# Mean squares of the prompt's heads on eight columns, and the sample's value sums stacked in one bank

## The chip, the cores and the metric

The kernel runs on one core of a Trainium2 chip. The metric is the time of one execution on the device, in microseconds. One layer of a decoder is computed for 256 prompt tokens and 8 sample tokens (264 in all) with the same weights.

## The reference, cut to what matters

The change touches two pieces: the RMS normalisation of the prompt's differential attention, and the sums of attention weights times cached values for the eight samples.

```python
def _diff_attend(q, k, v, q_pos, k_pos, lam, lam_init, subln_g):
    ...
    attn = p[:, :, 0] - lam * p[:, :, 1]
    o = jnp.einsum('bhqk,bkhe->bqhe', attn.astype(v.dtype), v).astype(jnp.float32)
    o = o * lax.rsqrt(jnp.mean(o * o, -1, keepdims=True) + RMS_EPS) * subln_g * (1.0 - lam_init)
    return o.astype(v.dtype)
...
def _layer_tail(x, a, o, ga, gb, w_a_up, w_b_up, w_out, ...):
    merged = jax.nn.sigmoid(ga) * (a @ w_a_up) + jax.nn.sigmoid(gb) * (o @ w_b_up)
    h = _layer_norm(ALPHA * x + merged @ w_out, ln1_g, ln1_b)
```

There are 4 differential heads of 128 values each. A sample attends to 256 cached keys in 2 pages and to its own new key.

## The kernel before, in words

Activations lie transposed: 128 features of a tile on the partitions, tokens along the columns. The order on each engine is written out by hand, and semaphores join the engines. Work runs in stages: 30 tiles of the input projection, the attention of prompt and samples with 16 gate tiles between its parts, the up projections, the output projection, a layer norm, and then the PEER experts (128 tiles of `experts_u`, 128 of `experts_v`), which are most of the time.

Attention writes to three PSUM banks in rotation. `UNIT_ORDER` lists the units; unit n uses bank 5 + n modulo 3. On TensorE `fill(name)` waits until the unit three before it has been copied out; `await_unit` and `await_drained` are the other sides of it. The stage of the change is this, in TensorE's order:

- gate tiles 14 and 15 (L1334), then 24 transposes of the sparse attention (L1453, six units that ScalarE copies out at L627), then the sparse value products of the prompt (L1467, L1469), copied out at L632.
- `sampT`: the samples' attention weights are transposed (L1496, L1498). VectorE copies them into `samp_pad` (L1019), where each sample has 32 columns of its own, eight of them filled.
- `rms0`, `rms1` (L1505): a 128x128 matrix of ones times the squares of `o_diff` (made by ScalarE at L663), 512 columns each. Every partition then holds the sum for each head and token. VectorE adds epsilon (L1039), takes the reciprocal over all 1024 columns (L1063), ScalarE takes the root (L687), VectorE multiplies (L1047) and scales (L1048).
- `samp_diff0`, `samp_diff1`, `samp_sparse0`, `samp_sparse1` (L1517): four samples per unit, each on 32 columns of the array, writing 32 partitions of the bank. `pick` (L1055) masks each out of its bank, and `samp_o` (L1527) turns the rows back into columns: 16 products with 8 columns.
- `rms2` (L1533): the same normalisation for the eight samples, 32 columns.
- the up projections (L1545, L1546, L1549), from `sparse_hi`, `sparse_lo`, `diff_hi`, `diff_lo`, which hold a rounded part and the rest (`diff_hi` at L689, `sparse_lo` at L1075, `diff_lo` at L1082), and from `up_hi`, `up_lo` (L678, L1069).

On VectorE the queue after `sampT` is: evacuate rms0 and rms1, reciprocal, `up_low` twice, `sparse_lo`, `pick(0)`, multiply, scale, `diff_lo`, `pick(1)`, and the samples' short steps. On ScalarE: the samples' exponentials (L615), two output copies, `up_high` twice, `sparse_hi`, root, `diff_hi`. GpSimd issues the loads of value pages (L449).

A product of two float32 operands shows as two matmul records in the trace, a transpose as one.

Of the kernel before, what the change touches and what calls it, by code (L numbers as in the profile page):

```python
# [27 lines left out]
ALU = mybir.AluOpType  # L28
ACT = mybir.ActivationFunctionType
# [47 lines left out]
CONSTS = C_OWNER + 2 * TS  # L77
# [21 lines left out]
              + [f"diffT{u}" for u in range(3)] + ["diff_o0", "diff_o1"]  # L99
# [9 lines left out]
def build_program(nc, x_t, weights, experts_u, experts_v, k_cache, v_cache,  # L109
                  page_table, sub_keys, params, consts, alibi, sample_bias, kv_out, y_out):  # L110
    with ExitStack() as ctx:
# [9 lines left out]
        def rounded(name, over, at, words):  # L121
# [9 lines left out]
            pad_zero pad_filled out_sample_ready rms_square rms_recip rms_root up_b_filled up_b_free  # L131
# [89 lines left out]
        samp_rows = s_sparse[:, 1024:3072].rearrange("p (n h e) -> p n h e", n=2, h=2)  # L221
# [22 lines left out]
        top8 = c(3 * 8)  # L244
        phase = c.at
# [313 lines left out]
        def _(act):  # L559
# [120 lines left out]

            up_high(0, 0)
# [4 lines left out]
            act.wait_ge(S["rms_recip"], 1)  # L686
            act.activation(s_diff[:, RMS:RMS + 4 * TP], s_diff[:, RMS:RMS + 4 * TP], ACT.Sqrt).then_inc(S["rms_root"], 1)  # L687
# [140 lines left out]
        def _(dve):  # L828
# [163 lines left out]

            dve.wait_ge(S["sample_scored"], 2)
# [43 lines left out]
            def mean_squares(u, at, n):  # L1037
                await_unit(dve, f"rms{u}")
                drain_unit(dve.tensor_scalar(s_diff[:, RMS + at:RMS + at + n], bank(f"rms{u}")[:, 0:n], 1.0 / P, EPS,  # L1039
                                             ALU.mult, ALU.add), f"rms{u}")  # L1040
                await_drained(dve, f"rms{u}")

            def rms_apply(t0, t1):

                o = o_diff[:, :, t0:t1]
                roots = s_diff[:, RMS + 4 * t0:RMS + 4 * t1].rearrange("p (j t) -> p j t", j=4)
                chain(dve.tensor_tensor(o, o, roots, ALU.mult))  # L1047
                chain(dve.tensor_scalar(o, o, par[:, P_SUBLN:P_SUBLN + 1], 1.0 - LAM_INIT, ALU.mult, ALU.mult))  # L1048

            def pick(n, kind, mask, heads):  # L1050

                for g in range(2):
                    name = f"samp_{kind}{g}"
                    await_unit(dve, name)
                    drain_unit(dve.tensor_tensor(samp_rows[:, n, g, :].rearrange("p (h e) -> p h e", h=heads),  # L1055
                                                 bank(name).rearrange("p (h e) -> p h e", h=heads),
                                                 cst[:, mask:mask + heads].unsqueeze(2).to_broadcast([P, heads, 512 // heads]),
                                                 ALU.mult), name)
# [19 lines left out]
            dve.wait_ge(S["rms_root"], 1)  # L1078
            rms_apply(0, TP)
# [18 lines left out]
            mean_squares(2, 4 * TP, 4 * TS)  # L1098
            dve.reciprocal(s_diff[:, RMS + 4 * TP:RMS + 4 * T], s_diff[:, RMS + 4 * TP:RMS + 4 * T])\
                .then_inc(S["rms_recip"], 1)  # L1100
            dve.wait_ge(S["rms_root"], 2)
            rms_apply(TP, T)
# [221 lines left out]
        def _(pe):  # L1324
# [159 lines left out]
            gate_tile(EARLY_GATES + 3)  # L1484
            pe.wait_ge(S["sparse_attn"], 2)
# [22 lines left out]
            for n, kind in enumerate(("diff", "sparse")):  # L1508
                pe.wait_ge(S["pad_filled"], 2 * n + 2)
                for h in range(2):  # L1510
                    name = f"samp_{kind}{h}"
                    fill(name)
                    for b in range(4 * h, 4 * h + 4):
                        pe.wait_ge(vc_loaded[b], 32)
                    for g in range(PAGES):
                        for q in range(4):
                            last = pe.matmul(bank(name)[32 * q:32 * q + 32, :], samp_pad[:, n, g, 4 * h + q, :],  # L1517
                                             vbuf[4 * h + q][kind][:, g, :], start=(g == 0), stop=(g == PAGES - 1))
                    last.then_inc(S["unit_filled"], 1)

            fill("samp_o")
            for n, kind in enumerate(("diff", "sparse")):
                for h in range(2):
                    await_drained(pe, f"samp_{kind}{h}")
                for j in range(4):
                    for h in range(2):
                        last = pe.matmul(bank("samp_o")[:, 32 * n + 8 * j:32 * n + 8 * (j + 1)],  # L1527
                                         samp_rows[:, n, h, j * P:(j + 1) * P], cst[:, C_OWNER + TS * h:C_OWNER + TS * (h + 1)],
# [272 lines left out]
```

## Time and profile before

| | |
|---|---|
| median of 3 runs | 1243.46 us |
| lowest, highest | 1240.25, 1245.73 us |
| profiled execution, its time | 1244.86 us |
| profiled execution, its span | 1242.9 us |
| mean granted TensorE clock | 0.97 |
| TensorE matmul busy | 1165.0 us, 94% |
| VectorE, ScalarE, GpSimd busy | 829.7, 524.8, 448.7 us |

Times of rows are in microseconds from the span's start. A granted clock of 1.00 is 2.4 GHz and 0.50 is 1.2 GHz. Busy time of TensorE comes from modelled ends of pipelined matmuls, so the distance between starts says more than the duration of one.

### The profile page before, as it was taken

The page shows a single profiled execution, that of the slowest core. Times are in us where ns is not written, and L with a number is a line of the kernel's source. Part 1 is how long each engine was busy: PE and PEld are TensorE (multiplying, and loading weights), DVE is VectorE, ACT ScalarE, POOL GpSimd, SP SyncE. Part 2 cuts the span into 40 slices and gives each one's busy share as a digit, 9 for nine tenths or more (in the row PEclk, how much of TensorE's full clock was granted, in tenths as well). Part 3 has the DMA queues.
Part 4 walks back from the last instruction along what each step waited for, and adds up shares of the span by engine and source line. Part 5 has one row for each costly group of instructions (what it writes and reads, how often), then busy time and mean ns, then how long its engine had stood idle before and what let it go on. Part 6 is the DMA issues. An engine that isn't in the chain of part 4 may idle for free.

```text
span 1242.9 us, 25892 instructions
## 1 busy us (share of the span) xinstructions
PE 1165.0 (94%) x9133; PEld 1113.8 (90%) x9133; DVE 829.7 (67%) x1827; ACT 524.8 (42%) x822; POOL 448.7 (36%) x237
## 2 busy tenths in 40 slices
PE   7998879799699999999999999999999999999996
PEld 7996756388599999989999999998999999999995
DVE  4447716546599999975666677746666666666665
ACT  4445224424334666765444444443333333333333
POOL 1100224022366999996666666663000000000000
PEclk9998897879899999999999999999999999999999
DMA  7772666314133454544334434444555555555551
GB/s 250 250 283 115 215 217 237 101 56 158 58 136 134 156 176 159 185 153 152 136 135 136 138 138 142 140 138 166 179 177 185 176 179 186 174 180 184 174 182 35
DMA packets 55175, 201.08 MB, mean 162 GB/s; under 512 B 6208, under 2 KB 7232, under 8 KB 54752
## 3 DMA queue, kind: packets, MB, share of 16 engines
q1 hardware_dynamic: 49472, 177.30, 41.4%
q0 software_dynamic: 5376, 23.01, 5.6%
q8 instruction: 17, 0.28, 0.1%
q10 hardware_dynamic: 288, 0.32, 0.1%
q14 instruction: 22, 0.18, 0.0%
HBM read 197.22 MB, written 3.38 MB: 161 GB/s over the span
## 4 chain that ended last, share of the span: by engine, by line
PE 79%; issue 7%; POOL 6%; DVE 6%; ACT 2%; POOLq 0%; DMA 0%; ACTq 0%; DVEq 0%
PE psum L1673 20%; PE psum L1682 10%; PE psum L1615 8%; PE psum L1610 7%; PE psum L1611 7%; POOL w_lo L548 5%; PE psum L1644 5%; PE psum L1350 5%; PE psum L1354 4%; PE psum L1351 4%; PE psum L1334 1%; PE psum L1389 1%; PE psum L1591 1%; PE psum L1570 1%; PE psum L1549 1%
## 5 line engine op out<-in xcount | busy, mean ns | idle before, releaser
L548 POOL TENSOR_TENSOR w_lo<-ring,w_hi 128x1024 fp32r<-128x1024 f32 x128 | 335.9, 2632 | 116.4 <-ACT w_hi L767 116.3
L1610 PE MATMUL psum<-h_hi,w_hi 128*128 128x264 f32 x1024 | 260.6, 290 | 0.0
L1673 PE MATMUL psum<-cells_hi,w_hi 128*128 128x264 f32 x1024 | 254.8, 285 | 3.0 <-ACT w_hi L814 3.0
L1611 PE MATMUL psum<-h_lo,w_hi 128*128 128x264 f32 x1024 | 254.6, 285 | 0.0
L1673 PE MATMUL psum<-cells_lo,w_hi 128*128 128x264 f32 x1024 | 254.5, 284 | 0.0
L814 ACT ACTIVATE w_hi<-ring 128x1024 fp32r<-128x1024 f32 x128 | 135.7, 1061 | 235.4 <-PE psum L1673 235.2
L767 ACT ACTIVATE w_hi<-ring 128x1024 fp32r<-128x1024 f32 x128 | 135.4, 1059 | 170.3 <-PE psum L1611 135.0
L1673 PEld LDWEIGHTS psum<-cells_hi,w_hi 128*128 128x128 f32 x1024 | 193.1, 189 | 3.3 <-issue 2.9
L1673 PEld LDWEIGHTS psum<-cells_lo,w_hi 128*128 128x128 f32 x1024 | 193.4, 189 | 0.0
L1611 PEld LDWEIGHTS psum<-h_lo,w_hi 128*128 128x128 f32 x1024 | 193.2, 189 | 0.0
L1610 PEld LDWEIGHTS psum<-h_hi,w_hi 128*128 128x128 f32 x1024 | 192.9, 188 | 0.3 <-issue 0.2
L1300 DVE TENSOR_TENSOR w_lo<-ring,w_hi 128x1024 fp32r<-128x1024 f32 x128 | 157.0, 1227 | 0.0
L1615 PE MATMUL psum<-h_hi,w_lo 128*128 128x264 f32 x1024 | 147.7, 286 | 8.9 <-POOL w_lo L548 8.7
L1615 PEld LDWEIGHTS psum<-h_hi,w_lo 128*128 128x128 f32 x1024 | 133.9, 189 | 11.6 <-POOL w_lo L548 11.6
L1682 PE MATMUL psum<-cells_hi,w_lo 128*128 128x264 f32 x1016 | 144.1, 284 | 0.0
L522 POOL TENSOR_TENSOR ring<-ring,small 128x264 f32<-128x264 f32 x4 | 3.0, 785 | 380.8 <-ACT small L719 380.8
L1682 PEld LDWEIGHTS psum<-cells_hi,w_lo 128*128 128x128 f32 x1016 | 132.0, 189 | 0.0
L1291 DVE CAST cells_hi<-arena 128x264 fp32r (+1 forms) x128 | 39.8, 311 | 125.8 <-PE psum L1682 125.8
L1350 PE MATMUL psum<-x_hi,z_hi 128*128 128x264 f32 x336 | 87.5, 295 | 10.0 <-DVE x_lo L838 8.6
L1257 DVE TENSOR_SCALAR work<-psum,work 128x128 f32<-128x128 f32 x264 | 89.7, 401 | 0.0
L1351 PE MATMUL psum<-x_lo,z_hi 128*128 128x264 f32 x336 | 85.1, 288 | 0.0
L1350 PEld LDWEIGHTS psum<-x_hi,z_hi 128*128 128x128 f32 x336 | 64.5, 192 | 14.6 <-ACT z_hi L576 8.6
(258 smaller groups left out, 1795.5 us busy)
## 6 DMA issues: line engine op xcount, KB each, us to landing
ring<-experts_u_dram SPq DMA_DIRECT2D x128, 512.0 KB, 3.2
ring<-experts_v_dram SPq DMA_DIRECT2D x128, 512.0 KB, 3.2
ring<-weights_dram SPq DMA_DIRECT2D x78, 512.0 KB, 3.4
arena<-k_cache_dram POOLq DMA_DIRECT2D x16, 576.0 KB, 6.3
arena<-v_cache_dram POOLq DMA_DIRECT2D x16, 512.0 KB, 7.4
kv_out_dram<-arena POOLq DMA_DIRECT2D x1, 2244.0 KB, 8.3
arena<-alibi_dram POOLq DMA_DIRECT2D x1, 1664.0 KB, 8.7
xt<-x_t_dram SPq DMA_DIRECT2D x2, 528.0 KB, 5.8
```

Of the source, the lines that this page charges most:

```text
L548: pool.tensor_tensor(halves_of(w_lo, k, D), raw, halves_of(w_hi, k, D), ALU.subtract)\
L767: act.activation(halves_of(w_hi, k, D), raw, ACT.Copy).then_inc(S["u_hi_made"], 1)
L814: act.activation(halves_of(w_hi, k, D), raw, ACT.Copy).then_inc(S["v_hi_made"], 1)
L1257: last = dve.tensor_scalar(p2[:, 4 * q + k, :], iota_near, slots[:, 1, t0 + k:t0 + k + 1], slots[:, 2, t0 + k:t0 + k + 1], ALU.is_equal, A ...
L1300: dve.tensor_tensor(halves_of(w_lo, k, D), raw, halves_of(w_hi, k, D), ALU.subtract)\
L1350: pe.matmul(out, part(hi, c, P), token_part(x_parts[0], c), start=(c == 0), stop=False)
L1351: pe.matmul(out, part(hi, c, P), token_part(x_parts[1], c), start=False, stop=False)
L1610: pe.matmul(out, part(hi, c, P), token_part(h_hi, c), start=(c == 0), stop=False)
L1611: last = pe.matmul(out, part(hi, c, P), token_part(h_lo, c), start=False, stop=False)
L1615: last = pe.matmul(out, part(lo, c, P), token_part(h_hi, c), start=False, stop=(c == DC - 1))
L1673: last = pe.matmul(psum[:, c, 0:T], part(hi, c, P), cells[n], start=(first and n == 0), stop=False)
L1682: last = pe.matmul(psum[:, c, 0:T], part(halves_of(w_lo, k, D), c, P), cell_part(cells_hi, k), start=False, stop=False)
```

## The change

The squares of `o_diff` become the stationary operand and a single column of ones the moving one. For each of 8 blocks of 128 (4 heads, 2 halves of the tokens) this gives one column, a sum per token on the partitions. The unit `rms0` now stands ahead of the sparse transposes. VectorE adds epsilon on 8 columns, ScalarE takes the root of 8, VectorE the reciprocal. To get the factor onto every partition, VectorE makes 8 diagonal blocks, the identity times the factor (128x1024, `rms_diag`), and TensorE multiplies them with ones (`spread0`, `spread1`); VectorE multiplies `o_diff` with the banks directly. The root stands ahead of `up_high` in ScalarE's queue, and the drain of `rms0` ahead of the sample's maxima (L995) in VectorE's.

In `samp_pad` the second four samples fill columns 8 to 15 of their 32, and both groups of four add up in one bank: two units in place of four, the same number of products, `pick` twice in place of four times, `samp_o` with 8 products in place of 16. `samp_diff` waits for the pages of all eight samples.

```diff
-              + ["sampT", "rms0", "rms1", "samp_diff0", "samp_diff1", "samp_sparse0", "samp_sparse1",
-                 "samp_o", "rms2"])
+              + ["sampT", "samp_diff", "spread0", "spread1", "samp_sparse", "samp_o", "rms2"])
...
# ScalarE
+            act.wait_ge(S["rms_recip"], 1)
+            act.activation(rms8, rms8, ACT.Sqrt).then_inc(S["rms_root"], 1)
             up_high(0, 0)
             up_high(0, 1)
...
-            act.wait_ge(S["rms_recip"], 1)
-            act.activation(s_diff[:, RMS:RMS + 4 * TP], s_diff[:, RMS:RMS + 4 * TP], ACT.Sqrt).then_inc(S["rms_root"], 1)
...
# VectorE, ahead of the sample's maxima
+            await_unit(dve, "rms0")
+            drain_unit(dve.tensor_scalar(rms8, bank("rms0")[:, 0:8], 1.0 / P, EPS, ALU.mult, ALU.add), "rms0")
+            await_drained(dve, "rms0")
+            dve.sem_inc(S["rms_recip"], 1)
...
-                    dve.tensor_copy(samp_pad[:, n, :, 4 * g:4 * g + 4, 0:8], pages).then_inc(S["pad_filled"], 1)
+                    dve.tensor_copy(samp_pad[:, n, :, 4 * g:4 * g + 4, 8 * g:8 * g + 8], pages).then_inc(S["pad_filled"], 1)
...
-            for u in range(2):
-                mean_squares(u, 512 * u, 512)
-            dve.reciprocal(s_diff[:, RMS:RMS + 4 * TP], s_diff[:, RMS:RMS + 4 * TP]).then_inc(S["rms_recip"], 1)
+            dve.wait_ge(S["rms_root"], 1)
+            chain(dve.reciprocal(rms8, rms8))
+            dve.tensor_tensor(rms_diag, ident.unsqueeze(1).to_broadcast([P, 8, P]),
+                              rms8.unsqueeze(2).to_broadcast([P, 8, P]), ALU.mult).then_inc(S["rms_spread"], 1)
...
-            dve.wait_ge(S["rms_root"], 1)
-            rms_apply(0, TP)
+            for u in range(2):
+                await_unit(dve, f"spread{u}")
+                o = o_diff[:, 2 * u:2 * u + 2, 0:TP]
+                drain_unit(dve.tensor_tensor(o, o, bank(f"spread{u}").rearrange("p (j t) -> p j t", j=2), ALU.mult), f"spread{u}")
+            for u in range(2):
+                await_drained(dve, f"spread{u}")
+            rms_scale(o_diff[:, :, 0:TP])
...
# TensorE, after gate tile 15
+            pe.wait_ge(S["rms_square"], 1)
+            fill("rms0")
+            for n in range(8):
+                last = pe.matmul(bank("rms0")[:, n:n + 1], s_diff[:, n * P:(n + 1) * P], ones[:, 0:1], start=True, stop=True)
+            last.then_inc(S["unit_filled"], 1)
...
# TensorE, after sampT
-            pe.wait_ge(S["rms_square"], 1)
-            for u in range(2):
-                fill(f"rms{u}")
-                pe.matmul(bank(f"rms{u}"), ones, s_diff[:, 512 * u:512 * (u + 1)], start=True, stop=True)\
-                    .then_inc(S["unit_filled"], 1)
+            def sample_values(n, kind):
+                name = f"samp_{kind}"
                 pe.wait_ge(S["pad_filled"], 2 * n + 2)
+                fill(name)
+                for b in range(TS):
+                    pe.wait_ge(vc_loaded[b], 32)
                 for h in range(2):
                     for g in range(PAGES):
                         for q in range(4):
                             last = pe.matmul(bank(name)[32 * q:32 * q + 32, :], samp_pad[:, n, g, 4 * h + q, :],
+                                             vbuf[4 * h + q][kind][:, g, :], start=(h == 0 and g == 0),
+                                             stop=(h == 1 and g == PAGES - 1))
+                last.then_inc(S["unit_filled"], 1)
+            sample_values(0, "diff")
+            pe.wait_ge(S["rms_spread"], 1)
+            for u in range(2):
+                fill(f"spread{u}")
+                pe.matmul(bank(f"spread{u}"), ones, rms_diag[:, 4 * u:4 * u + 4, :].rearrange("p n q -> p (n q)"),
+                          start=True, stop=True).then_inc(S["unit_filled"], 1)
+            sample_values(1, "sparse")
...
-                    for h in range(2):
-                        last = pe.matmul(bank("samp_o")[:, 32 * n + 8 * j:32 * n + 8 * (j + 1)],
-                                         samp_rows[:, n, h, j * P:(j + 1) * P], cst[:, C_OWNER + TS * h:C_OWNER + TS * (h + 1)],
-                                         start=(h == 0), stop=(h == 1))
+                    last = pe.matmul(bank("samp_o")[:, 32 * n + 8 * j:32 * n + 8 * (j + 1)],
+                                     samp_rows[:, n, j * P:(j + 1) * P], cst[:, C_OWNER:C_OWNER + TS], start=True, stop=True)
```

The masks `C_PAIR`, `C_HEAD` and `C_OWNER` move with the rows, and `rms_apply` loses its first part to the lines above.

## Rows read from the trace of the kernel before

**Rows 1.** The page, part 1: busy time by engine.
```profile
PE 1165.0 (94%) x9133; PEld 1113.8 (90%) x9133; DVE 829.7 (67%) x1827; ACT 524.8 (42%) x822; POOL 448.7 (36%) x237
```

**Rows 2.** The chain of waits, 214 to 228: start, us, what.
```profile
214.24 7.32 PE psum L1334 x32
...
222.03 3.04 ACT work L627 x6
...
227.51 0.17 DVE small L1001
```

**Rows 3.** Timeline of TensorE: start, us, instructions, idle before.
```profile
221.39 2.92 PE L1453 MATMUL psum<-cst,work 128*128 128x128 f32 x24
225.13 0.66 PE L1467 MATMUL psum<-work 128*64 128x256 f32 x4 [0.81 <-ACT work L627]
...
227.56 0.44 PE L1469 MATMUL psum<-work 128*64 128x128 f32 x4
229.37 0.34 PE L1496 MATMUL psum<-cst,small 64*128 64x64 f32 x2 [1.37 <-DVE small L1010]
...
231.38 3.78 PE L1505 MATMUL psum<-arena,cst 128*128 128x512 f32 x4 [1.10 <-DVE small L1024]
235.09 6.52 PE L1517 MATMUL psum<-arena,work 128*32 128x512 f32 x48
246.54 3.64 PE L1517 MATMUL psum<-arena,work 128*32 128x512 f32 x16 [4.93 <-DVE work L1055]
250.12 7.00 PE L1527 MATMUL psum<-cst,work 128*128 128x8 f32 x32
...
260.39 0.59 PE L1545 MATMUL psum<-sparse_hi,up_hi 128*128 128x264 f32 x1 [1.82 <-DVEq L1110]
```

**Rows 4.** Timeline of VectorE, 231 to 250.
```profile
231.49 0.43 DVE L1034 TENSOR_TENSOR small<-small,arena 64x32 f32<-64x32 f32 x2
...
235.99 6.55 DVE L1063 RECIPROCAL arena<-arena 128x1024 f32<-128x1024 f32 x1
242.46 2.29 DVE L1069 TENSOR_TENSOR up_lo<-ring,up_hi 128x1024 fp32r<-128x1024 f32 x2
244.67 1.22 DVE L1075 TENSOR_TENSOR sparse_lo<-arena,sparse_hi 128x1024 fp32r<-128x1024 f32 x1
245.81 1.28 DVE L1055 TENSOR_TENSOR work<-psum,cst 128x512 f32<-128x512 f32 x2
247.01 1.22 DVE L1047 TENSOR_TENSOR arena<-arena 128x1024 f32<-128x1024 f32 x1
248.26 0.75 DVE L1048 TENSOR_SCALAR arena<-arena,par 128x1024 f32<-128x1024 f32 x1
```

**Rows 5.** Windows of 1 us: busy by engine, TensorE's granted clock third from last.
```profile
121.00:122.00 1.00, 0.53 (x4) 0.00 (x0) 1.00 (x2) 1.00 (x3) 0.00 (x0) 0.79 0.00 0
230.00:231.00 1.00, 0.28 (x3) 0.14 (x2) 0.68 (x5) 1.00 (x2) 0.00 (x0) 0.83 0.56 213
237.00:238.00 1.00, 1.00 (x12) 0.12 (x4) 1.00 (x1) 0.00 (x0) 0.00 (x0) 0.76 0.00 0
244.00:245.00 1.00, 0.00 (x0) 0.00 (x0) 1.00 (x2) 0.00 (x0) 0.00 (x0) 0.65 0.30 53
250.00:251.00 1.00, 1.00 (x9) 0.89 (x5) 0.81 (x1) 0.16 (x1) 0.00 (x0) 0.50 0.00 0
264.00:265.00 1.00, 1.00 (x7) 1.00 (x6) 0.12 (x1) 0.00 (x0) 0.00 (x0) 0.61 0.00 0
```

**Rows 6.** Timeline of VectorE, the sample's maxima.
```profile
214.28 0.42 DVE L995 SCALAR_TENSOR_TENSOR small<-psum,sbias 64x257 f32<-64x257 f32 x1 [2.03 <-PE psum L1480]
```

**Rows 7.** Timeline of ScalarE.
```profile
231.48 1.28 ACT L687 ACT_TABLE_LOAD   x1
...
249.10 1.06 ACT L689 ACTIVATE diff_hi<-arena 128x1024 fp32r<-128x1024 f32 x1 [5.46 <-DVEq L1080]
```

**Rows 8.** Timeline of GpSimd, the last value page issued.
```profile
204.55 0.72 POOL L449 DMA_DIRECT2D arena<-v_cache_dram  x1 [0.41 <-issue]
```

More of the change, by code:

```diff
@@ L98 @@
               + [f"diff{u}" for u in range(6)] + ["isum"] + [f"sparse{u}" for u in range(6)]
[L99 removed]
+              + [f"diffT{u}" for u in range(3)] + ["diff_o0", "diff_o1", "rms0"]
               + [f"sparseT{u}" for u in range(6)] + ["sparse_o0", "sparse_o1"]
[L101 to L102 removed]
+              + ["sampT", "samp_diff", "spread0", "spread1", "samp_sparse", "samp_o", "rms2"])
 UNIT = {name: n for n, name in enumerate(UNIT_ORDER)}
@@ L1035, in _, with rms_scale @@
             chain.settle()
[L1037 to L1047, printed above, removed]
+            def rms_scale(o):
                 chain(dve.tensor_scalar(o, o, par[:, P_SUBLN:P_SUBLN + 1], 1.0 - LAM_INIT, ALU.mult, ALU.mult))
             def pick(n, kind, mask, heads):
[L1052 to L1058, printed above, removed]
-            for u in range(2):
-                mean_squares(u, 512 * u, 512)
-            dve.reciprocal(s_diff[:, RMS:RMS + 4 * TP], s_diff[:, RMS:RMS + 4 * TP]).then_inc(S["rms_recip"], 1)
+                name = f"samp_{kind}"
+                await_unit(dve, name)
+                drain_unit(dve.tensor_tensor(samp_rows[:, n, :].rearrange("p (h e) -> p h e", h=heads),
+                                             bank(name).rearrange("p (h e) -> p h e", h=heads),
+                                             cst[:, mask:mask + heads].unsqueeze(2).to_broadcast([P, heads, 512 // heads]),
+                                             ALU.mult), name)
+            dve.wait_ge(S["rms_root"], 1)
+            chain(dve.reciprocal(rms8, rms8))
+            dve.tensor_tensor(rms_diag, ident.unsqueeze(1).to_broadcast([P, 8, P]),
+                              rms8.unsqueeze(2).to_broadcast([P, 8, P]), ALU.mult).then_inc(S["rms_spread"], 1)
             def up_low(i, m):
@@ L1097, in _ @@
                               ALU.subtract).then_inc(S["sparse_lo_made"], 1)
-            mean_squares(2, 4 * TP, 4 * TS)
-            dve.reciprocal(s_diff[:, RMS + 4 * TP:RMS + 4 * T], s_diff[:, RMS + 4 * TP:RMS + 4 * T])\
-                .then_inc(S["rms_recip"], 1)
+            roots = s_diff[:, RMS + 4 * TP:RMS + 4 * T]
+            await_unit(dve, "rms2")
+            drain_unit(dve.tensor_scalar(roots, bank("rms2")[:, 0:4 * TS], 1.0 / P, EPS, ALU.mult, ALU.add), "rms2")
+            await_drained(dve, "rms2")
+            dve.reciprocal(roots, roots).then_inc(S["rms_recip"], 1)
             dve.wait_ge(S["rms_root"], 2)
-            rms_apply(TP, T)
+            o = o_diff[:, :, TP:T]
+            chain(dve.tensor_tensor(o, o, roots.rearrange("p (j t) -> p j t", j=4), ALU.mult))
+            rms_scale(o)
             dve.sem_inc(S["out_sample_ready"], 1)
@@ L1501, in _ @@
             await_drained(pe, "sampT")
-            pe.wait_ge(S["rms_square"], 1)
-            for u in range(2):
-                fill(f"rms{u}")
-                pe.matmul(bank(f"rms{u}"), ones, s_diff[:, 512 * u:512 * (u + 1)], start=True, stop=True)\
-                    .then_inc(S["unit_filled"], 1)
-            for n, kind in enumerate(("diff", "sparse")):
+            def sample_values(n, kind):
+                name = f"samp_{kind}"
                 pe.wait_ge(S["pad_filled"], 2 * n + 2)
+                fill(name)
+                for b in range(TS):
+                    pe.wait_ge(vc_loaded[b], 32)
                 for h in range(2):
[L1511 to L1514, printed above, removed]
                     for g in range(PAGES):
```

19 lines of the change are left out of this document (9 added, 10 removed).

## The prediction

> **What bounds the kernel now.** The page's first part comes first: TensorE is busy for 94% of the span and no other engine for more than 67% [rows 1]. So outside its own waits a change pays only through what TensorE has to do, and inside them through what it waits for. The chain of waits around the edit shows the order of events: gate tile 15 ends at 221.56, the sparse transposes follow, ScalarE copies six units, loads a table and does the sample's exponentials, and VectorE takes over at 227.51 [rows 2]. The timeline of TensorE then shows the stage itself. The sample transposes start at 229.37. After them come the two rms products of 512 columns (231.38 to 235.09), the diff value sums and the first half of the sparse ones (235.09, for 6.52 us), an idle 4.93 us that a copy by VectorE at L1055 ends, the last 16 value instructions (3.64 us), the 32 instructions of samp_o (7.00 us), rms2, and at 260.39 the first up product [rows 3]. From 231.38 to 260.39 is 29.0 us. VectorE's timeline says why TensorE idles: between the first rms product and the copy that frees the bank lies the reciprocal over 1024 columns, 6.55 us, with up_low and sparse_lo behind it [rows 4]. The bank rotation carries the wait: samp_sparse1 needs samp_diff1 drained, and pick(0, "diff") is queued behind the reciprocal on VectorE. The granted clock is the last view: each row is a mean of the two levels 1.00 (2.4 GHz) and 0.50 (1.2 GHz), so its share dates the step. It falls at 230.7, rises at 237.5, falls again at 244.3 inside the idle stretch, samp_o begins at 0.50, and it rises at 264.8, after the up products have begun [rows 5].
>
> **The change, part by part, on the path.**
>
> *Added ahead of the stage.* The mean squares now take 8 products of one column each, with 128x128 stationary slices, between gate tile 15 and the sparse transposes. That place is on the chain [rows 2], so all of their time counts. The nearest row is samp_o: 16 products of 8 columns are 32 instructions in 7.00 us, 0.219 us each at half clock, where weight loads of 128x128 fill the time [rows 3, 5]. The clock at 221 is full, so I take half, 0.11 us, for 16 instructions: 1.7 us. Transposes at full clock give 2.9 us / 24 = 0.12 [rows 3], 1.9 us. Bounds: 0 (if hidden behind ScalarE's evacuation of the gate) and 3.5 us (half clock). VectorE's drain of 8 columns comes next, some 0.2 us (the reciprocal of two columns takes 0.17 [rows 2]); it is over before the third transpose unit wants its bank, since ScalarE takes 3.04 us for the six units [rows 2]. VectorE had nothing to do there but the sample's maxima (from L995 on, four instructions of about 0.4 us, before at 214.28 [rows 6]); they move to about 225.2. ScalarE wants them after its copies and table load, at 221.56, plus 1.7, four transposes (0.5), 3.04 and 1.28, which is 228.1 [rows 2, 3, 7]. Cover is 2.9 us; without it the difference would be paid in full. So everything to the start of the stage shifts by 1.7, and 231.38 becomes 233.1.
>
> The Trainium skill ("TensorE: Matmul & The Clock Gate", section "Back-to-back issue gap") gives small products a floor of about 25 ns from start to start, and adds that in streams with weight loads the spacing is set by both. By the floor alone the 16 instructions would be an estimated 0.4 us instead of 1.7. Samp_o's row speaks against it: 0.219 us for 8 columns.
>
> *TensorE in the stage.* The rms products at its head go (3.71 us). Then:
> - samp_diff, now 32 instructions in a row. At half clock they take 3.64 / 16 = 0.227 us each by the last row of them [rows 3], so 0.113 at full clock. When does the clock rise? Before it took 6.1 us from 231.38, and 4.4 us from 260.39 [rows 3, 5]; I take 5.2: 23 instructions, then 9 at 0.113, in all 6.2 us. It ends at 239.3.
> - spread0 and spread1: 4 instructions of 512 columns, before 0.93 each at half clock (3.71 / 4), so 0.45 at full: 1.8 us, to 241.1. They wait for rms_spread. VectorE makes it from a reciprocal of 8 columns (0.2) and a product of 128x1024 (1.22, as L1047 [rows 4]) right after its small sample work at 231.92 + 1.7; done at 235.1, 4 us before it is wanted. Its root on ScalarE needs the table load, 1.28 [rows 7], now ahead of up_high: up_hi and sparse_hi come some 1.5 us later, and VectorE reaches up_low only at 235.1. Nothing is late.
> - samp_sparse, 32 x 0.113 = 3.6, to 244.7. Its bank needs the diff copy: VectorE has done up_low (2.29) and sparse_lo (1.22) at 238.6, then copies samp_diff at 239.3 to 240.0.
> - samp_o: 8 products in place of 16, 16 instructions at full clock. Half (0.9 us) can run once samp_sparse is issued, the other half waits for pick(1).
>
> *VectorE in the stage.* Gone: the reciprocal (6.55), two evacuations of 512 columns and their waits, two of four copies of 0.64, one product of 1.22. New: 0.2, 1.22, and two products of 128x512 out of the bank of about 0.64 each (as L1055 [rows 4]). From spread1 at 241.1: product 0.64, scale 0.75, diff_hi on ScalarE 1.1, diff_lo 1.2 (as sparse_lo), pick(1) 0.64 [rows 4, 7]: 245.6. This chain now sets the end, 0.9 us past TensorE. With the last 8 instructions of samp_o (0.9) it is 246.5.
>
> *Tail.* From samp_o's end to the first up product was 257.12 to 260.39, 3.27 us of short steps [rows 3]. It is not edited: 249.8.
>
> **The sum.** 260.39 - 249.8 = 10.6 us. In parts: TensorE's stage to the end of samp_o is 13.4 instead of 25.7 us, 12.3 less; 1.7 is given back ahead of it. The up products follow and everything after waits for TensorE or for what TensorE releases; no transfer with a clock of its own is in the chain, so I carry the gain to the end. The profiled execution took 1244.86 us with a span of 1242.9; 1244.9 - 10.6 = 1234.3. The median of the runs is 1243.46, 1.4 below it, so 1233 is my time, 0.85% less.
>
> **Rivals.**
> 1. *The clock falls before the stage.* Between gate tile 15 and the sparse value products (L1467) TensorE now has 5.3 us of one-column products and transposes, before 3.6. After 3 us of idling in two places (227.9 to 230.7, 241.6 to 244.4) it fell [rows 3, 5]. If it falls here, the products of 2.9 us take up to twice that, of which 1.4 us fit before the sample transposes: 1.5 us lost, and samp_diff may start colder. Against: the clock held through 24 transposes. Time 1235 to 1236.
> 2. *The clock does not rise during the value sums.* They use 32 columns of the array at a time, and the 3.64 us of them at 246.54 raised nothing [rows 3, 5]. Then samp_diff takes 7.3, spread 3.7, samp_sparse 7.3 from 233.1 to 251.4; with the copy (0.64) and half of samp_o (1.75) it is 253.8, the up products start at 257.1, a gain of 3.3: 1240. Against: the earlier scores of the same 128x32 form (L1429) had it rise at 121.4 [rows 5], and here the stretch is longer and without a gap.
> 3. *The clock is still full at the first up product.* Before, 4.4 us of them ran at half, so up to 2.2 us more: 1231. Against: the samp_o products at half clock and the waits of the tail never raised it, and here the tail still idles.
> 4. *Small products are nearly free*, as the floor would have it: 1.3 us less ahead, 0.7 less in samp_o: 1231. For it nothing in the rows. This is the rule weighed above.
> 5. *It does nothing in the end*: the stage is shorter, but a later wait on something other than TensorE takes it back. 1243. VectorE at 67% and ScalarE at 42% leave room [rows 1].
> 6. *Slower: the wait for all eight value pages.* samp_diff now waits for pages 0 to 7 at once. The last page is issued at 204.55 [rows 8] and nothing wants it before 231. If it landed after 233.1, each us would be paid; the gain is gone at 243.7 and a slowdown of 0.5% begins at 249.9. A landing at 252 would give 1252. Against: 28 us of lead.
>
> **How the numbers follow.** Forecast 0.61; rival 1 0.13, rival 2 0.07, rival 3 0.08, rival 4 0.03, rival 5 0.05, rival 6 0.03. The forecast's own range is 1230.5 to 1236 (the clock's rise between 4.4 and 6.1 us is 0.9 us, the added products -1.7 to +1.8 of their 1.7, runs before spread over 5.5 us). The range takes in rivals 1, 3 and 4 and the way to rival 2: 1229 to 1239, and leaves out some 1.5 in 10. A measurement of this kernel tells 0.5%, 6.2 us, from no change, so faster is below 1237.2: forecast, rivals 1, 3 and 4 almost whole, 0.82; the same is rivals 2 and 5 and a rest, 0.14; slower 0.04.
>
> **What would show it.** Right: L1063 gone with its 6.55 us, no idle of more than 0.5 us on TensorE between the sample transposes and samp_o, samp_o in 16 instructions near 0.11 us, the first up product near 249.8, and the same distance from there to the end as before. The added products show as 16 instructions of one column at 221.6, 0.11 us each. Wrong if the clock in 234 to 245 stays at 0.50, if L1467 after them runs at half, if the table load or the maxima hold up ScalarE at 228, or if the up products start earlier and a later wait grows.

## Result and the profile after

| | before | changed |
|---|---|---|
| median (11 runs each) | 1242.76 us | 1231.9 us |
| lowest, highest | 1239.6, 1248.3 | 1229.7, 1237.65 |
| ratio, 95% interval | | 0.9919 [0.9899, 0.9939] |
| span of the profiled execution | 1242.9 | 1227.7 |

The change makes the kernel 0.8% faster; 1233 us was forecast. The two profiled spans differ by more, 15.2 us. Where that comes from is read off three marks that both traces have: the first product of gate tile 14, the first up product, and the first product of the output projection.

| stretch | before | changed | difference |
|---|---|---|---|
| start to gate tile 14 | 214.17 | 209.22 | -4.95 |
| gate tile 14 to the first up product | 46.22 | 34.96 | -11.26 |
| to the output projection | 29.89 | 30.22 | +0.33 |
| to the end | 952.6 | 953.3 | +0.7 |

The first stretch holds no edited line. In the twelve traces of this study (these two and one of each experiment) gate tile 14 begins anywhere from 208.66 to 215.07, whatever was edited behind it. So 4.95 us of the 15.2 is luck of these two executions, and the medians of the runs rightly differ by less. The edit's part is 10.9 us up to the output projection.

The timeline of TensorE in the changed kernel: start, us, line, what; L1493 is the unit of one-column products, L1521 the value sums, L1530 the spread products, L1538 samp_o, L1543 rms2.
```profile
209.22 7.39 PE L1339 MATMUL psum<-xt,ring 128*128 128x264 f32 x32
216.44 1.84 PE L1493 MATMUL psum<-cst,arena 128*128 128x1 f32 x16
218.15 2.96 PE L1458 MATMUL psum<-cst,work 128*128 128x128 f32 x24
...
226.16 0.34 PE L1506 MATMUL psum<-cst,small 64*128 64x64 f32 x2 [1.37 <-DVE small L1016]
...
228.17 5.34 PE L1521 MATMUL psum<-arena,work 128*32 128x512 f32 x32 [1.10 <-DVE small L1030]
233.44 1.99 PE L1530 MATMUL psum<-arena,cst 128*128 128x512 f32 x4
235.35 3.64 PE L1521 MATMUL psum<-arena,work 128*32 128x512 f32 x32
238.93 2.20 PE L1538 MATMUL psum<-cst,work 128*128 128x8 f32 x16
241.95 0.41 PE L1543 MATMUL psum<-arena,cst 128*128 128x32 f32 x2 [0.83 <-ACT arena L693]
244.18 0.59 PE L1555 MATMUL psum<-sparse_hi,up_hi 128*128 128x264 f32 x1 [1.82 <-DVEq L1115]
```
The idle 4.93 us of [rows 3] is gone, and so are the two rms products at the head of the stage. From the start of samp_diff to the end of samp_o nothing on TensorE waits longer than a fraction of a microsecond. Samp_o is 16 instructions in 2.20 us at full clock, a short wait between its halves included, where it was 32 in 7.00 at half.

The chain of waits of the changed kernel over the end of the stage shows what sets its end now.
```profile
233.50 1.93 PE psum L1530 x4
...
235.46 0.70 DVE arena L1077
...
236.25 0.76 DVE arena L1044
...
237.10 1.07 ACT diff_hi L690
...
238.19 0.94 DVE diff_lo L1083
...
239.33 0.69 DVE work L1050
...
240.07 1.07 PE psum L1538 x8
```
After the second spread product the chain leaves TensorE. It runs over VectorE's product and scale, ScalarE's diff_hi, diff_lo and the copy of samp_sparse, and returns for the second half of samp_o.

The granted clock of the changed kernel, third number from the end of each window of 1 us:
```profile
228.00:229.00 1.00, 0.83 (x8) 0.29 (x12) 0.87 (x6) 1.00 (x2) 0.00 (x0) 0.91 1.00 426
232.00:233.00 1.00, 1.00 (x16) 0.18 (x8) 1.00 (x2) 0.00 (x0) 0.00 (x0) 0.88 0.47 152
242.00:243.00 1.00, 0.36 (x2) 0.25 (x2) 0.74 (x3) 0.02 (x1) 0.00 (x0) 0.74 0.00 0
249.00:250.00 1.00, 1.00 (x9) 1.00 (x9) 0.07 (x1) 0.00 (x0) 0.00 (x0) 0.85 0.00 0
```
Read as in [rows 5], it falls at 228.8, when samp_diff has run for 0.65 us, rises at 232.2 (4.1 us into samp_diff), falls at 242.5 in the tail and rises at 249.3, which is 5.1 us after the first up product, against 4.4 before. Those 0.7 us more at half clock cost half their length, the +0.33 of the table. The second fall of before, at 244.3, has no counterpart: it happened in the idle time that is gone, and had put the last 16 value instructions and all of samp_o at half clock.

### The profile page after: what moved, and what is told of

Same layout as the page of the kernel before. It is cut to its first block, busy times and chain, and to the rows that moved or that the text cites. A ratio compares the mean times of both kernels' runs of the same rounds, so it can differ in the third digit from the quotient of the medians.

```text
span 1227.7 us, 25892 instructions
## 1 busy us (share of the span) xinstructions
PE 1158.3 (94%) x9133; PEld 1111.8 (91%) x9133; DVE 822.4 (67%) x1826; ACT 523.9 (43%) x822; POOL 448.1 (37%) x237
## 4 chain that ended last, share of the span: by engine, by line
PE 80%; issue 8%; POOL 6%; DVE 4%; ACT 2%; POOLq 0%; DMA 0%; ACTq 0%; DVEq 0%
PE psum L1683 20%; PE psum L1692 10%; PE psum L1625 8%; PE psum L1620 7%; PE psum L1621 7%; POOL w_lo L549 5%; PE psum L1355 5%; PE psum L1654 5%; PE psum L1356 4%; PE psum L1359 4%; PE psum L1339 1%; PE psum L1601 1%; PE psum L1394 1%; PE psum L1580 1%; PE psum L1559 1%
```

## The experiments

All distances are in microseconds from the first product of gate tile 14, in one profiled execution of each kernel. That makes them independent of the first stretch. The changed kernel, e1 and e7 have the same code up to the value sums and agree to 0.01 us there. A step of the clock that falls elsewhere can move a distance by more, up to 1.8 us in e2, so each is read together with the clock. The ratios are to the kernel before, from runs on the same chip. The intervals of e1, e3 to e6 and e8 overlap that of the changed kernel, so how those differ from it is read from the distances alone. "Up" is the first up product, "output" the first product of the output projection. In the kernel before and in e2 the two rms products stand ahead of the value sums. Where gate tile 15 was moved away, gate tile 14 is the first half of the old row L1339.

| kernel | value sums begin | up | output | ratio [95%] |
|---|---|---|---|---|
| before | 20.92 | 46.22 | 76.11 | |
| changed | 18.95 | 34.96 | 65.18 | 0.9919 [0.9899, 0.9939] |
| e1, rms part alone | 18.95 | 36.74 | 66.23 | 0.9935 [0.9910, 0.9961] |
| e2, stacking alone | 19.12 | 40.66 | 71.00 | 0.9975 [0.9954, 0.9996] |
| e3, rms0 in the gap | 17.64 | 33.45 | 63.10 | 0.9903 [0.9874, 0.9932] |
| e4, extra products | 19.42 | 34.70 | 62.64 | 0.9901 [0.9872, 0.9930] |
| e5, gate tile 15 later | 18.36 | 33.00 | 62.64 | 0.9891 [0.9859, 0.9923] |
| e6, e3 and extra products | 17.65 | 32.93 | 60.87 | 0.9885 [0.9852, 0.9918] |
| e7, copy first | 18.95 | 34.72 | 65.06 | profile only |
| e8, e5 and extra products | 18.31 | 32.95 | 60.78 | 0.9882 [0.9846, 0.9919] |
| e9, e8 with rms0 earlier | 16.24 | 30.88 | 58.74 | 0.9863 [0.9839, 0.9888] |
| e10, e9 and copy first | 16.24 | 30.63 | 58.46 | 0.9871 [0.9847, 0.9894] |

**e1: the rms part alone.** The changed kernel with the sample's part as it was:
```diff
-                    dve.tensor_copy(samp_pad[:, n, :, 4 * g:4 * g + 4, 8 * g:8 * g + 8], pages).then_inc(S["pad_filled"], 1)
+                    dve.tensor_copy(samp_pad[:, n, :, 4 * g:4 * g + 4, 0:8], pages).then_inc(S["pad_filled"], 1)
...
+                for h in range(2):
+                    name = f"samp_{kind}{h}"
+                    fill(name)
...
+                    for h in range(2):
+                        last = pe.matmul(bank("samp_o")[:, 32 * n + 8 * j:32 * n + 8 * (j + 1)],
+                                         samp_rows[:, n, h, j * P:(j + 1) * P], cst[:, C_OWNER + TS * h:C_OWNER + TS * (h + 1)],
+                                         start=(h == 0), stop=(h == 1))
```


> The mean squares on 8 columns with the spread product, but the sample's value sums in four units and samp_o with 16 products as before. Distances are measured from the first product of gate tile 14 to the first up product: 46.2 us in the kernel before, 35.0 in the changed one. My theory (the reciprocal over 1024 columns held the bank and with it TensorE, and is most of the gain): VectorE has two more copies of 0.64 us and samp_o 16 instructions more, of which half or so lie on the path, so 37.0 us, a gain of 9 over the kernel before, ratio 0.993. Rival (stacking is most of the gain, because it takes two bank waits away): 42 us or more, ratio 0.997.

Measured: 36.74 us, 9.5 less than before. The timeline of TensorE in e1:
```profile
230.10 5.34 PE L1522 MATMUL psum<-arena,work 128*32 128x512 f32 x32 [1.10 <-DVE small L1030]
235.36 1.99 PE L1530 MATMUL psum<-arena,cst 128*128 128x512 f32 x4
237.28 3.65 PE L1522 MATMUL psum<-arena,work 128*32 128x512 f32 x32
240.86 3.75 PE L1540 MATMUL psum<-cst,work 128*128 128x8 f32 x32
```
The four units run without a wait between them. Without the reciprocal, the bank rotation of before costs nothing. The clock matters too: the same 32 instructions of samp_o took 7.00 us at half clock in the kernel before and 3.75 here, so 3.3 of the 9.5 us come from a clock that no longer falls ahead of them.

What stacking adds is 1.8 us. Samp_o begins 10.76 us after the value sums in both kernels and ends 1.55 us later in e1, whose chain of waits stays on TensorE:
```profile
237.35 3.58 PE psum L1522 x32
240.93 3.70 PE psum L1540 x32
```
So VectorE's two extra copies are covered here. The other 0.23 us are in the tail: rms2 runs at half clock in e1 (0.63 us) and at full in the changed kernel (0.41 us).

**e2: the stacking alone**, on the kernel before:
```diff
-                for h in range(2):
-                    name = f"samp_{kind}{h}"
-                    fill(name)
...
+                name = f"samp_{kind}"
+                fill(name)
+                for b in range(TS):
+                    pe.wait_ge(vc_loaded[b], 32)
...
-                    for h in range(2):
-                        last = pe.matmul(bank("samp_o")[:, 32 * n + 8 * j:32 * n + 8 * (j + 1)],
-                                         samp_rows[:, n, h, j * P:(j + 1) * P], cst[:, C_OWNER + TS * h:C_OWNER + TS * (h + 1)],
-                                         start=(h == 0), stop=(h == 1))
+                    last = pe.matmul(bank("samp_o")[:, 32 * n + 8 * j:32 * n + 8 * (j + 1)],
+                                     samp_rows[:, n, j * P:(j + 1) * P], cst[:, C_OWNER:C_OWNER + TS], start=True, stop=True)
```


> The value sums stacked in one bank per kind and samp_o with 8 products, but the mean squares by two products of 512 columns and the reciprocal over 1024 columns as before. My theory: TensorE no longer waits for the copy behind the reciprocal and is through its value sums at about 243.4 on the clock of the kernel before, but VectorE's row of reciprocal, up_low, sparse_lo, copy, product, scale, diff_lo and copy then sets the end: 42.3 us from gate tile 14 to the first up product, a gain of 4, ratio 0.997. The two parts would then gain 9 and 4 alone and 11.3 together. Rival (the two parts are independent and add up): 44 us, a gain of 2.

Measured: 40.66 us, 5.6 less than before. Neither number fits, the forecast was 42.3. TensorE's timeline and a window of e2:
```profile
228.14 1.99 PE L1504 MATMUL psum<-arena,cst 128*128 128x512 f32 x4 [1.10 <-DVE small L1024]
230.06 7.08 PE L1516 MATMUL psum<-arena,work 128*32 128x512 f32 x64
241.61 1.85 PE L1525 MATMUL psum<-cst,work 128*128 128x8 f32 x8 [4.47 <-DVE work L1054]
246.44 1.87 PE L1525 MATMUL psum<-cst,work 128*128 128x8 f32 x8 [2.99 <-DVE work L1054]
```
```profile
239.00:240.00 1.00, 0.00 (x0) 0.00 (x0) 1.00 (x2) 0.00 (x0) 0.00 (x0) 0.95 0.27 90
```
The mechanism is as expected: all 64 value instructions in one go, then TensorE waits twice for VectorE's copies. The size is off because in this execution the clock stayed at 1.00 from before sampT to 239.9. The rms products took 1.99 us and not 3.78, so the reciprocal began 1.8 us earlier, counted from gate tile 14. Those 1.8 us are luck of this execution: with them it would have been an estimated 42.5, near the forecast, and the twelve runs show 3.1 us less than before (0.5 to 5.7 by the interval). So the parts gain 9.5 and about 4 alone (5.6 in this trace) and 11.3 together. The sum of the parts is more than the whole because both remove the same idle time.

**e3: the one-column products in a gap.** From ahead of the sparse transposes to behind the sparse value products, where TensorE waited for the sample's chain; in `UNIT_ORDER` "rms0" moves to between "sparse_o1" and "sampT", and VectorE drains it ahead of its wait for sampT:
```diff
-            pe.wait_ge(S["rms_square"], 1)
-            fill("rms0")
-            for n in range(8):
-                last = pe.matmul(bank("rms0")[:, n:n + 1], s_diff[:, n * P:(n + 1) * P], ones[:, 0:1], start=True, stop=True)
-            last.then_inc(S["unit_filled"], 1)
             pe.wait_ge(S["sparse_attn"], 2)
...
             outputs("sparse", 8, HD)
+            pe.wait_ge(S["rms_square"], 1)
+            fill("rms0")
+            for n in range(8):
+                last = pe.matmul(bank("rms0")[:, n:n + 1], s_diff[:, n * P:(n + 1) * P], ones[:, 0:1], start=True, stop=True)
+            last.then_inc(S["unit_filled"], 1)
```


> The changed kernel with the eight one-column products moved behind the sparse value products of the prompt, where TensorE stood idle for 1.81 us before the sample transposes, and VectorE's drain of them ahead of its wait for sampT. My theory (their 1.7 us ahead of the sparse transposes are paid in full): 33.3 us from gate tile 14 to the first up product, 1.7 less than the changed kernel; over the kernel before a gain near 12.5, ratio 0.990. Rival (the products delay the sample transposes or the root on ScalarE comes too late for the diagonal blocks): 34.5 or more.

Measured: 33.45 us, 1.51 less than the changed kernel, 1.7 expected. The timeline of TensorE in e3:
```profile
227.15 0.44 PE L1474 MATMUL psum<-work 128*64 128x128 f32 x4
227.52 1.95 PE L1498 MATMUL psum<-cst,arena 128*128 128x1 f32 x16
229.39 0.33 PE L1506 MATMUL psum<-cst,small 64*128 64x64 f32 x2
...
231.40 4.91 PE L1521 MATMUL psum<-arena,work 128*32 128x512 f32 x32 [1.10 <-DVE small L1030]
```
The products fill the gap of 1.81 us and hold the sample transposes up by 0.43 (15.63 from gate tile 14, 15.20 in the kernel before). So the move itself gains 1.31 us, the difference at the start of the value sums, and not 1.7. The total comes closer by luck: the clock rose 2.6 us into samp_diff (at 234.0) and not 4.1, which takes 0.43 off, and rms2 at half clock puts 0.23 back.

**e4: what the half clock costs.** Six products that nobody reads, into a bank that is unused in this stage:
```diff
+            def warm(count):
+                for _ in range(count):
+                    pe.matmul(psum[:, 4, :], ones, cst[:, 0:512], start=True, stop=True)
+            warm(2)
             pe.wait_ge(S["samp_attn"], 2)
...
+            warm(1)
             await_drained(pe, "sampT")
...
+            warm(1)
             pe.wait_ge(S["rms_square"], 2)
...
+            warm(2)
             pe.wait_ge(S["sparse_lo_made"], 2)
```


> The changed kernel with six extra products of 512 columns whose result nobody reads, two ahead of the sample transposes, one ahead of the value sums, one behind samp_o and two ahead of the first up product; they fill TensorE's idle times. Nothing that the kernel needs is changed. It measures what the half clock costs in this stage. My theory: the value sums run at full clock from the start (3.6 us in place of 5.3), but VectorE's up_low and sparse_lo then hold the chain, so only 0.6 us of it reaches the first up product; the first up products run at full clock too, 2.5 us less. From gate tile 14 to the first product of the output projection 62.2 us against 65.2 in the changed kernel. Rival (the clock falls all the same in the tail, or the extra products delay the short steps): 64.5 to 66.

Measured: 62.64 us to the output projection, 2.54 less than the changed kernel. In its timeline the value sums take 3.64 us in place of 5.34. They begin 0.47 us later than in the changed kernel, because the two extra products ahead of the sample transposes hold those up. Then TensorE waits 0.59 us ahead of samp_sparse:
```profile
233.38 3.64 PE L1528 MATMUL psum<-arena,work 128*32 128x512 f32 x32
236.95 1.99 PE L1537 MATMUL psum<-arena,cst 128*128 128x512 f32 x4
239.53 3.64 PE L1528 MATMUL psum<-arena,work 128*32 128x512 f32 x32 [0.59 <-issue]
```
The row names no releaser. Samp_sparse needs the bank of samp_diff, and VectorE's timeline has the copy that frees it (L1050) behind sparse_lo, ending at 239.43. So it is VectorE, as forecast:
```profile
237.61 1.22 DVE L1071 TENSOR_TENSOR sparse_lo<-arena,sparse_hi 128x1024 fp32r<-128x1024 f32 x1
238.75 0.68 DVE L1050 TENSOR_TENSOR work<-psum,cst 128x512 f32<-128x512 f32 x1
```
The first up product gains only 0.26; the rest is the up products at full clock. The clock is 1.00 in every window from 225 to 262. (The trace had 954.6 us from there to the end, 1.3 more than the changed kernel, so the ratio shows less. That stretch varied from 950.1 to 955.5 over the twelve traces.)

**e5: gate tile 15 into the gap**, on e3:
```diff
             gate_tile(EARLY_GATES + 2)
-            gate_tile(EARLY_GATES + 3)
...
+            gate_tile(EARLY_GATES + 3)
             await_drained(pe, "sampT")
...
# ScalarE
-            evac_gate(EARLY_GATES + 3)
...
+            evac_gate(EARLY_GATES + 3)
             act.wait_ge(S["diff_normed"], 1)
```


> The kernel of e3 with gate tile 15 moved behind sampT on TensorE, and its sigmoid on ScalarE behind sparse_hi. The gate tile (3.66 us) no longer stands ahead of the sparse transposes, and fills the time in which TensorE waited for sampT's copies and VectorE worked through up_low. My theory (the stage is a chain of short steps with TensorE free in between, so real work belongs there): the value sums start at 16.5 us from the first product of gate tile 14 in place of 17.6 and run at full clock, 31.0 us to the first up product in place of 33.45, 60.6 to the output projection in place of 63.1; ratio to the kernel before 0.988. Rival (the extra table loads for the late sigmoid delay ScalarE's steps in the tail, or VectorE's chain is the bound and not TensorE): 33 us or more to the first up product.

Measured: 33.0 us. My theory missed by 2. The timeline of TensorE and two windows of e5:
```profile
225.27 1.95 PE L1497 MATMUL psum<-cst,arena 128*128 128x1 f32 x16
...
227.99 5.51 PE L1339 MATMUL psum<-xt,ring 128*128 128x264 f32 x16
233.43 3.64 PE L1521 MATMUL psum<-arena,work 128*32 128x512 f32 x32
```
```profile
228.00:229.00 1.00, 1.00 (x4) 0.86 (x4) 0.87 (x6) 1.00 (x2) 0.00 (x0) 0.65 1.01 426
231.00:232.00 1.00, 1.00 (x4) 0.83 (x3) 1.00 (x2) 0.86 (x1) 0.00 (x0) 0.65 0.00 0
```
The clock fell at 228.3, as the gate tile began, and came back at 231.7. The tile took 5.5 us and not 3.7, and the value sums waited for it. So the rival's number came true, but hardly for its reasons. VectorE was idle for 2.55 us before its copy of samp_diff, so it was not the bound. The late sigmoid does put a table load of 1.28 us into the chain of the tail, and by the lengths of the tails it costs 0.1 us here and 0.3 in e8 (3.37 us from the end of samp_o to the first up product, 3.06 in e6).

**e6: e3 with four extra products.** As e4, without the two ahead of the sample transposes.

> The kernel of e3 with the four later extra products of e4: one ahead of the value sums, one behind samp_o and two ahead of the first up product, none ahead of the sample transposes. My theory (what e4 gained, it gained in the tail, where the up products then start at full clock): 33.3 us from gate tile 14 to the first up product as in e3, and 60.8 to the output projection in place of 63.1; ratio 0.988. Rival (the one-column products ahead of the sample transposes do not hold the clock and the extra products behind samp_o alone cannot either, so that it falls in the tail): 62.5 to 63.2.

Measured: 32.93 and 60.87; 33.3 and 60.8 were expected. With products in the tail's gaps the clock stays at 1.00 through the up products; the three in the tail are enough, as e8 shows.

The start of the stage in e6 bears on e5. From the end of the last value product of the prompt (225.94) to the first wide product behind it, the extra one, TensorE has the same 2.6 us of one-column products and sample transposes as e5 has ahead of gate tile 15. Here the clock did not fall:
```profile
225.50 0.44 PE L1474 MATMUL psum<-work 128*64 128x128 f32 x4
225.87 1.95 PE L1498 MATMUL psum<-cst,arena 128*128 128x1 f32 x16
...
228.58 1.13 PE L1504 MATMUL psum<-cst 128*128 128x512 f32 x2
```
```profile
228.00:229.00 1.00, 1.00 (x9) 0.81 (x8) 0.33 (x4) 0.89 (x2) 0.00 (x0) 1.00 0.54 205
```

**e7: the copy first**, on the changed kernel:
```diff
             dve.sem_inc(S["diff_normed"], 1)
+            pick(1, "sparse", C_HEAD, 8)
             dve.wait_ge(S["diff_hi_made"], 1)
             dve.tensor_tensor(token_cols(diff_lo, 0, TP), o_diff[:, :, 0:TP], token_cols(diff_hi, 0, TP), ALU.subtract)\
                 .then_inc(S["diff_lo_made"], 1)
-            pick(1, "sparse", C_HEAD, 8)
```


> The changed kernel with VectorE's copy of samp_sparse moved ahead of its wait for diff_hi, so that it runs before diff_lo. My theory (at the end of the stage VectorE's chain from spread1 through scale, diff_hi, diff_lo and the copy is what samp_o waits for): the copy starts when samp_sparse is filled, 0.3 to 0.4 us earlier than now, diff_lo moves behind it beside samp_o, and the first up product comes at 34.6 to 34.7 us from gate tile 14 in place of 34.96; diff_lo then ends before samp_o does. Rival (TensorE's own row sets the end): 34.96 as it is.

Measured: 34.72, 0.24 less. VectorE's timeline in e7:
```profile
238.51 0.69 DVE L1050 TENSOR_TENSOR work<-psum,cst 128x512 f32<-128x512 f32 x1 [2.06 <-PE psum L1521]
239.12 1.22 DVE L1084 TENSOR_TENSOR diff_lo<-arena,diff_hi 128x1024 fp32r<-128x1024 f32 x1
240.36 0.19 DVE L1092 TENSOR_TENSOR arena<-psum,small 128x32 f32<-128x32 f32 x1
```
The copy now waits for TensorE, and the next short step stands behind diff_lo in VectorE's queue. VectorE's chain was the last by a quarter of a microsecond and no more.

**e8: e5 with three extra products in the tail.**

> The kernel of e5 with the three extra products in the tail (one behind samp_o, two ahead of the first up product), as in e6. My theory: both gains add up, 31.0 us from gate tile 14 to the first up product and 58.5 to the output projection, against 46.2 and 76.1 in the kernel before; the rest of the kernel unchanged at 952 to 954 us; ratio to the kernel before 0.986. Rival (a later stage takes part of it back): the rest of the kernel grows by 1 us or more.

Measured: 32.95 and 60.78, the rest 954.3. Both effects add up (62.64 less 1.86), but from e5's lower start: gate tile 15 again took 5.46 us.

**e9: the one-column products between transposes and value products**, on e8:
```diff
             transposes("sparse", s_sparse, 8, lambda h: h)
+            pe.wait_ge(S["rms_square"], 1)
+            fill("rms0")
+            for n in range(8):
+                last = pe.matmul(bank("rms0")[:, n:n + 1], s_diff[:, n * P:(n + 1) * P], ones[:, 0:1], start=True, stop=True)
+            last.then_inc(S["unit_filled"], 1)
             await_drained(pe, "sparseT5")
             outputs("sparse", 8, HD)
-            pe.wait_ge(S["rms_square"], 1)
-            fill("rms0")
-            for n in range(8):
-                last = pe.matmul(bank("rms0")[:, n:n + 1], s_diff[:, n * P:(n + 1) * P], ones[:, 0:1], start=True, stop=True)
-            last.then_inc(S["unit_filled"], 1)
```


> The kernel of e8 with the eight one-column products taken out of the gap ahead of the sample transposes and put between the sparse transposes and the sparse value products, where TensorE waits 0.81 us for ScalarE's copies; VectorE drains them behind the sample's maxima. It asks why gate tile 15 took 5.4 us in e5 and e8 in place of 3.66 and came to be what the value sums wait for. My theory (the clock fell at 228.3 in e5 because the one-column products ahead of the sample transposes are followed by short steps; with the value products closer to the gate tile it stays full): gate tile 15 takes 3.7 us, the value sums start at 16.6 us from the first product of gate tile 14 in place of 18.3, the first up product comes at 31.2 in place of 32.95 and the output projection at 59.0 in place of 60.8. Rival (the clock falls all the same, since the chip sees one-column products and transposes as idling wherever they stand): 32.9 and 60.7, or later, with the sparse value products at half clock.

Measured: 16.24, 30.88 and 58.74, each within 0.4 of the theory. TensorE's timeline in e9:
```profile
215.85 1.92 PE L1494 MATMUL psum<-cst,arena 128*128 128x1 f32 x16
...
220.13 0.44 PE L1474 MATMUL psum<-work 128*64 128x128 f32 x4
220.99 0.33 PE L1505 MATMUL psum<-cst,small 64*128 64x64 f32 x2 [0.42 <-DVE small L1016]
...
221.82 3.83 PE L1339 MATMUL psum<-xt,ring 128*128 128x264 f32 x16
```
The gate tile takes 3.83 us, here and in e10, with the clock at 1.00; it took 5.51 and 5.46 in e5 and e8. Of the 2.07 us by which the value sums begin earlier than in e8, 1.63 are the gate tile and 0.44 the closed gap. Between the end of the last value product and the gate tile lie 1.3 us here and 2.7 in e5. The theory's numbers came true, but its reason is not shown: e6 has the order of e5 and held the clock, and e2 held it over 3.4 us. In the seven traces in which it fell at this place, it fell 2.6 to 4.2 us after the last value product. That fits a shorter stretch being safer, and no more.

**e10: e9 with the copy first.**

> The kernel of e9 with VectorE's copy of samp_sparse ahead of diff_lo, as in e7. Theory: it takes 0.25 us more off, as it did in the changed kernel, so 0.25 less than e9 to the first up product; ratio to the kernel before 0.985. Rival (TensorE with samp_sparse is the last in this order, since the value sums start earlier than VectorE's work ends): no difference from e9.

Measured: 30.63, 0.25 less, as expected. Its ratio lies inside e9's interval; 0.25 us is below what the runs tell. The intervals of e9 and e10 lie just below the changed kernel's 0.9919 [0.9899, 0.9939]; each is against the kernel before on its own chip.

## Why the prediction was right

It was right in sign, size and mechanism: e1 shows that the mean squares were most of it, and e2 that with the reciprocal in place TensorE still waits for VectorE. Point by point:

- *The added products, 1.7 us, in full on the chain*: 16 instructions from 216.61 to 218.29 in the chain, 1.68. The start of the stage moved by 1.74 (17.21 to 18.95). e3 took them off the chain and began the value sums 1.31 earlier. The pace is 0.105 us each. The floor of about 25 ns that the Trainium skill gives ("TensorE: Matmul & The Clock Gate", section "Back-to-back issue gap") is not what binds here. The remark in the same section of the Trainium skill that in a stream both operations set the spacing agrees with the trace: the sixteen weight loads lie back to back in 1.98 us. The Trainium skill (same page, section "LDWEIGHTS (loading the stationary operand)") gives columns / 1.2 in nanoseconds for a weight load, an estimated 107 for 128 columns. The trace agrees at full clock, and not at half, where [rows 3] have 0.219 us for each product with its weight load.
- *VectorE's maxima and ScalarE's table load are covered*: the maxima ended at 220.3, ScalarE wanted them at 223.2. The root ran at 226.73, VectorE used it at 228.75. The cover of 2.9 was right.
- *samp_diff 6.2 us*: 5.3. The clock was still full for its first 0.65 us, where the sum had it at half from the start, and it rose 4.1 us in and not 5.2. This is the term that was off most, by 0.9. The rise is a matter of the execution: it came 2.6 us into samp_diff in e3.
- *Spread 1.8*: 1.93. *samp_sparse 3.6*: 3.58. *VectorE's chain 4.5 from the second spread product*: 235.43 to 240.02, 4.6. *Last half of samp_o 0.9*: 1.07. *Tail 3.27*: 3.04, since rms2 ran at full clock.
- *10.6 us to the first up product*: 11.26, and 10.9 to the output projection. The medians differ by 10.9, the ratio says 10.1.

Of the rivals, the first (the clock falls ahead of the stage) did not occur in the changed kernel: it was 1.00 in each window from 218 to 228. But it fell at 228.8, right behind this place, and in e5 and e8, where gate tile 15 follows, it fell as early as 2.6 us after the last value product. The second (no rise during the value sums) is refuted by the window 232 to 233, the third (a warm tail) by the window 242 to 243; e4, e6 and e8 show what it would have paid, 1.9 to 2.5 us. The fourth is refuted by the pace of the one-column products. The fifth would need the gain to vanish after the output projection, and that stretch is the same within its scatter. For the sixth, samp_diff began on VectorE's copy and not on a page.

Two readings of the prediction were off without consequence. One of its signs asked for no idle time of more than 0.5 us on TensorE between the sample transposes and samp_o; the 1.10 us ahead of samp_diff, in which VectorE copies sampT, are as they were in the kernel before. And the idling from 227.9 to 230.7, behind which the clock fell, holds the sample transposes (229.37 to 230.28).

What stays open is the scatter of the parts that were not edited. The start of gate tile 14 moved by 6.4 us between executions, and the stretch from the output projection to the end by 5.4. The runs of one kernel spread over 8 us; no run shows the cause of either. Nor is it shown why the clock held in e9 and e10: there is one trace of each kernel, and e6 held it with the longer stretch of e5.

## What to carry to other kernels

A slow operation that sits between the filling and the draining of a rotating bank holds up whoever fills the bank next, even when its own result is wanted late. Shrinking its columns (1024 to 8 and a product to spread them) removed 6.6 us of VectorE and the idle time of TensorE behind it, and with the idle time a fall of the clock that had doubled the time of the work after it. New small work goes where its engine waits anyway: on the chain the one-column products cost 1.7 us, in the gap of e3 0.4. When a stage is a chain of short steps, ask of each gap whether the clock survives it, since the work behind it is what pays.

## What the runs showed of the hardware that was not expected

- The same gate tile took 3.83 us in e9 and e10 and 5.5 in e5 and e8. The difference between e8 and e9 is where 16 one-column instructions of 1.9 us stand, with their drain on VectorE; that this is the cause is not shown. In e5 and e8 TensorE was in use all the while before the clock fell (one-column products, then 64-column ones) and it fell nevertheless; in e6 the same instructions stood there and it did not fall.
- Samp_o's 8-column instructions take 0.219 us each at half clock and 0.116 at full (32 in 7.00 us before, 32 in 3.70 in e1). Their weight loads lie back to back, 32 in 6.90 us at half clock, and so do those of the one-column products of the changed kernel, 16 in 1.98 us at full:
```profile
250.12 6.90 PEld L1527 LDWEIGHTS psum<-cst,work 128*128 128x128 f32 x32 [1.66 <-issue]
```
```profile
216.22 1.98 PEld L1493 LDWEIGHTS psum<-cst,arena 128*128 128x128 f32 x16
```
- 7.00 us of samp_o at half clock did not raise the clock, nor did the 3.64 us of value sums right ahead of it [rows 3, 5]. At the head of the stage 4.1 us of value sums did in the changed kernel and 2.6 in e3. So the kind of work alone does not settle it either.
- In e2 the clock survived the wait for sampT's copies. It fell in that wait in the kernel before and in e3, and 0.65 to 0.8 us behind it in the changed kernel, e1 and e7. The wait itself was 1.10 us in each of them, so the state of the clock there is not settled by the order of the work alone.
